# Norm chain with fewer and reordered steps, and a shared area padded to a 128-byte base

## The chip, the cores and the metric

The kernel runs on one core of a Trainium2 chip. The metric is the device time of one execution in microseconds; the times given are medians of runs. The core has a matmul engine (TensorE, PE), a vector engine (DVE), a scalar engine (ACT), a GpSimd engine (POOL) and a sync engine (SP) whose queue issues most transfers. Each works through its own list of instructions in order and waits for the others by semaphores.

## The reference

Everything is float32, T = 512 tokens, width D = 1024. The first block has two layers; each layer has a feed-forward, a mixer and a feed-forward, each behind a norm, and a final norm follows. The second block has a hybrid of attention and a gated linear recurrence, and an MLP, each behind a norm.

```
rms_norm(x, g)       = x * rsqrt(mean(x * x, -1) + 1e-6) * g
modulate(h, sh, sc)  = h * (1 + sc) + sh            # sh, sc, gate from silu(c) @ ada_w + ada_b
swiglu(h)            = (silu(a) * b) @ w_out,  [a | b] = h @ w_in        # inner width 2816
layer 0: ffn, pool_mixer (trailing means over 2, 4, 8, 16 tokens, then a 256x256 map per group), ffn
layer 1: ffn, conv_mixer (h @ w_in, causal 3-tap convolution, @ w_out), ffn
x = x + 0.5 * gate * swiglu(modulate(rms_norm(x, g), sh, sc))            # the mixers: without 0.5
```

## The kernel before

Activations lie transposed: the residual `X` is eight tiles of 128 channels by 512 tokens, all in on-chip memory. Every product with a weight is exact float32 from three passes: weight and activation are each split into a rounded high half and the rest, and `products` issues high x high, high x low and low x high (L1382 to L1384). A *unit* of weights is up to 1024 rows by 256 columns. SP loads unit u into `W_RAW[u % 2]` once unit u-2 has been split (L393, L397); ACT rounds it into `W_HI` (`split_hi`, L529) once the products of unit u-2 are over; DVE subtracts (`split_lo`, L773) and so frees the raw buffer; PE multiplies. In a feed-forward a half is 11 input units and 8 output units (`IN_UNITS`, `OUT_UNITS`); each input unit has 48 products of 512 columns (8 tiles of `H_HI`, `H_LO` by 2 column blocks by 3 passes).

There are nine norms, r = 0 to 8: 0 ahead of the first feed-forward, 1 ahead of the pool mixer, 2, 3 ahead of feed-forwards, 4 ahead of the convolution, 5 ahead of the last feed-forward, 6 the final norm of the first block, 7 and 8 in the second block. A norm goes through four engines:

- ACT squares the eight tiles of `X` into two buffers (`squares`, L536); DVE copies the first into `SSQ` (L833) and adds the others (L836), each addition behind the one before. In front of norms 1, 3, 4 and 6 tiles 0 to 6 are squared and summed during the last two output units (`EARLY`); only tile 7 is left. In front of norms 5 and 8 two tiles are left, in norms 2 and 7 nearly all.
- PE reduces `SSQ` over channels: four column products of one column each (`norm`, L1394). They are plain float32 and appear as 8 instructions.
- ACT takes the root (`root`, L540). The table of the root and that of Silu are different ones; a table load of its own (ACT_TABLE_LOAD) precedes a function whose table isn't there.
- DVE takes the reciprocal (L841) and makes four diagonal tiles (L846); PE multiplies ones with them (L1397, two instructions), which spreads the 512 factors over all partitions.
- For each tile k DVE forms x * gain * factor into `GT[k % 2]` (`normed`, L852), ACT adds the shift into `SA[k % 2]` (L548) and rounds it into `H_HI` (L551), DVE subtracts into `H_LO` (`lo`, L859), and the first unit's products of tile k may start. DVE's order is normed 0, normed 1, lo 0, normed 2, lo 1, and so on.

The order around it is written by hand. The unit that the first products need is split already. The unit after it (`ahead`) is rounded by ACT between the last square and the root, and subtracted by DVE between the last sum and the reciprocal, in norms 2 to 5 and likewise in norm 1. In norm 1 DVE then shifts the tiles in place (L935), forms the trailing means (L944 to L956), splits them (L960), and adds the mixer's result to `X` (L876); PE starts the third of four groups (L1437) when the first group's addition is done. Ahead of norm 1's root ACT also takes Silu of the two other condition vectors (L592).

Many buffers of different stages share one area, `FLEX`, by offsets: `G_HI`, `G_LO`, `ADA`, `SA`, `GT`, `PH` and those of the second block.

## Time and profile before

| | us |
|---|---|
| median of three timed runs | 3264.14 |
| lowest and highest of them | 3259.08, 3264.15 |
| the profiled execution | 3260.7 |
| its span, first to last instruction | 3258.7 |
| busy in it: PE, DVE, ACT | 2849.9, 1579.4, 870.9 |

The mean granted clock of PE was 0.921 of full speed. Rows of the timeline give start, duration, engine, line and operation, and in brackets how long the engine had been idle before and who released it. PE's products overlap: one of 512 columns lasts longer than the distance to the next.

### The profile page before, as it was taken

How to read it: one execution, taken by the hardware profiler on the slowest of the kernel's cores; microseconds unless marked ns; L12 is line 12 of the kernel's file. 1: busy time of each engine (PE TensorE's matmuls, PEld its weight loads, DVE VectorE, ACT ScalarE, POOL GpSimd, SP SyncE). 2: the span in 40 equal slices, each digit the busy share in tenths (PEclk: the TensorE clock that was granted, in tenths of full speed). 3: DMA queues.
4: the chain of work that ended last, by engine and by line, in shares of the span. 5: the costliest groups of instructions: out<-in, count | busy, mean ns of one | idle time of the engine just before them, and what ended most of it. 6: DMA issues, size and time to landing. Idle time of an engine off the chain costs nothing.

```text
span 3258.7 us, 33240 instructions
## 1 busy us (share of the span) xinstructions
PE 2849.9 (87%) x12574; PEld 2321.7 (71%) x12574; DVE 1579.4 (48%) x2135; ACT 870.9 (27%) x937; POOL 65.6 (2%) x132
## 2 busy tenths in 40 slices
PE   4999939999899998989999478877666669989999
PEld 3888828888788887878887366766544448778887
DVE  5636476455563844556343555355323243354444
ACT  3212223221322223231222333333122243332221
POOL 0100000000000000000000000000000000000000
PEclk9999969999999999999999678877877789999999
DMA  6746415455373643236342201001100003323232
GB/s 235 233 121 207 123 51 167 150 162 189 92 238 107 214 128 85 96 97 213 109 131 75 63 27 39 27 27 42 31 13 13 13 26 90 90 78 100 93 103 78
DMA packets 418458, 340.17 MB, mean 104 GB/s; under 512 B 11328, under 2 KB 399936, under 8 KB 410048
## 3 DMA queue, kind: packets, MB, share of 16 engines
q1 hardware_dynamic: 400368, 244.84, 25.6%
q0 software_dynamic: 17568, 93.33, 7.7%
q8 instruction: 63, 1.03, 0.1%
q10 hardware_dynamic: 432, 0.75, 0.1%
q14 instruction: 27, 0.22, 0.0%
HBM read 336.78 MB, written 2.10 MB: 104 GB/s over the span
## 4 chain that ended last, share of the span: by engine, by line
PE 84%; DVE 9%; ACT 3%; issue 2%; SPq 1%; DMA 0%; DVEq 0%; ACTq 0%
PE ps L1382 23%; PE ps L1383 23%; PE ps L1384 23%; PE ps L1476 3%; PE ps L1478 3%; PE ps L1477 3%; PE ps L1650 2%; PE ps L1640 1%; DVE gla_kql L1154 1%; SPq L393 1%; DVE stat L1275 1%; ACT w_hi L529 1%; PE ps L1397 1%; DVE gla_el L1139 1%; DVE attn_p L1285 0%
## 5 line engine op out<-in xcount | busy, mean ns | idle before, releaser
L1382 PE MATMUL ps<-h_hi,w_hi 128*128 128x512 f32 x2256 | 894.2, 396 | 39.5 <-DVE h_lo L859 18.8
L1383 PE MATMUL ps<-h_lo,w_hi 128*128 128x512 f32 x2256 | 888.7, 394 | 0.0
L1384 PE MATMUL ps<-h_hi,w_lo 128*128 128x512 f32 x2256 | 887.8, 394 | 0.0
L773 DVE TENSOR_TENSOR w_lo<-w_raw,w_hi 128x2048 fp32r<-128x2048 f32 (+1 forms) x240 | 504.7, 2103 | 201.2 <-ACT w_hi L529 200.8
L529 ACT CAST w_hi<-w_raw 128x2048 fp32r<-128x2048 f32 (+1 forms) x240 | 421.9, 1758 | 617.0 <-PE ps L1384 554.4
L1382 PEld LDWEIGHTS ps<-h_hi,w_hi 128*128 128x128 f32 x2256 | 430.9, 191 | 147.8 <-issue 58.1
L1383 PEld LDWEIGHTS ps<-h_lo,w_hi 128*128 128x128 f32 x2256 | 430.7, 191 | 91.0 <-issue 1.5
L1384 PEld LDWEIGHTS ps<-h_hi,w_lo 128*128 128x128 f32 x2256 | 430.1, 191 | 91.2
L1382 PE MATMUL ps<-g_hi,w_hi 128*128 128x512 f32 x960 | 373.4, 389 | 0.0
L1383 PE MATMUL ps<-g_lo,w_hi 128*128 128x512 f32 x960 | 373.4, 389 | 0.0
L1384 PE MATMUL ps<-g_hi,w_lo 128*128 128x512 f32 x960 | 373.4, 389 | 0.0
L876 DVE SCALAR_TENSOR_TENSOR x_res<-ps,gate,x_res 128x512 f32<-128x512 f32 (+1 forms) x120 | 87.4, 749 | 401.3 <-PE ps L1384 395.2
L566 ACT ACTIVATE silu_a<-ps 128x512 f32<-128x512 f32 x88 | 52.7, 599 | 730.9 <-PE ps L1384 730.9
L891 DVE TENSOR_TENSOR g_t<-silu_a,ps 128x512 f32<-128x512 f32 x88 | 60.6, 688 | 360.8 <-ACT silu_a L566 360.8
L778 DVE SCALAR_TENSOR_TENSOR ada<-ada,cond 128x1024 f32<-128x1024 f32 x176 | 207.7, 1220 | 0.3 <-DMA ada<-in_ada_t 0.2
L1383 PEld LDWEIGHTS ps<-g_lo,w_hi 128*128 128x128 f32 x960 | 180.2, 188 | 37.5
L1384 PEld LDWEIGHTS ps<-g_hi,w_lo 128*128 128x128 f32 x960 | 180.2, 188 | 37.4
L1382 PEld LDWEIGHTS ps<-g_hi,w_hi 128*128 128x128 f32 x960 | 180.2, 188 | 37.3
L1558 PE MATMUL ps<-gla_kql 128*128 128x128 f32 x224 | 56.8, 439 | 38.5 <-DVE gla_kql L1154 38.5
L1558 PEld LDWEIGHTS ps<-gla_kql 128*128 128x128 f32 x224 | 49.7, 327 | 46.0 <-DVE gla_kql L1154 46.0
L1640 PE MATMUL ps<-ident,attn_p 128*128 128x128 f32 x192 | 37.5, 354 | 49.6 <-DVE attn_p L1285 49.6
L1394 PE MATMUL ps<-ones_d,ssq 128*128 128x1 f32 x72 | 14.3, 320 | 75.8 <-DVE ssq L836 75.8
(264 smaller groups left out, 2624.5 us busy)
## 6 DMA issues: line engine op xcount, KB each, us to landing
w_raw<-in_ffn_w_in SPq DMA_DIRECT2D x176, 512.0 KB, 5.0
ada<-in_ada_t POOLq DMA_DIRECT2D x56, 1024.0 KB, 6.5
ada<-in_ada_t POOLq DMA_DIRECT2D x64, 512.0 KB, 5.3
w_raw<-in_w_mlp SPq DMA_DIRECT2D x64, 512.0 KB, 4.3
w_raw<-in_w_in SPq DMA_DIRECT2D x52, 512.0 KB, 4.6
w_raw<-in_ffn_w_out SPq DMA_DIRECT2D x64, 384.0 KB, 4.1
w_raw<-in_ffn_w_out SPq DMA_DIRECT2D x64, 320.0 KB, 3.4
w_raw<-in_conv_w_in SPq DMA_DIRECT2D x24, 512.0 KB, 4.4
```

Source lines behind the costliest of these rows:

```text
L529: nc.scalar.copy(W_HI[u.slot][:, 0:n], W_RAW[u.slot][:, 0:n]).then_inc(hi_done, 1)
L773: nc.vector.tensor_tensor(W_LO[u.slot][:, 0:n], W_RAW[u.slot][:, 0:n], W_HI[u.slot][:, 0:n].bitcast(F32), ALU.subtract).then_inc(lo_done, 1)
L778: return nc.vector.scalar_tensor_tensor(tile, tile, 1.0, COND[cond][:], ALU.mult, ALU.mult, accum_out=MOD_SUMS[:, bass.ds(n.v, 1)])
L876: return nc.vector.scalar_tensor_tensor(x, bank[:], GATE[:, bass.ds((m + 8 * gate).v, 1)], x, ALU.mult, ALU.add)
L1382: pe.matmul(dst, hi[:, k, c], rhs_hi(k), start=(k == 0), stop=False)
L1383: pe.matmul(dst, hi[:, k, c], rhs_lo(k), start=False, stop=False)
L1384: last = pe.matmul(dst, lo[:, k, c], rhs_hi(k), start=False, stop=(k == kt - 1))
L1476: pe.matmul(dst, a_hi, b_hi, start=first, stop=False)
L1477: pe.matmul(dst, a_hi, b_lo, start=False, stop=False)
L1478: return pe.matmul(dst, a_lo, b_hi, start=False, stop=last)
L1558: last = pe.matmul(BANK[6 + n % 2][:, cc], KQL[n % 2][:, 0, cc], KQL[n % 2][:, 1, cc], start=True, stop=True)
L1640: last = pe.transpose(WIDE[2 * (c % 2)][:, t * P:(t + 1) * P], PP[c % 2][:, t * P:(t + 1) * P], IDENT[:])
```

## The change

1. The weight unit `ahead` is rounded by ACT behind tile 3 of the norm's loop, and subtracted by DVE behind normed 5 and lo 4. In norm 1 ACT takes the root first and then rounds; DVE subtracts behind the pool's last low half and ahead of the residual additions.
2. The first two squares are added in one operation (no copy), and tile 7 is left out of `SSQ`. PE multiplies `SSQ` (tiles 0 to 6) when it is ready, and then the square of tile 7 from its own buffer into the same columns: 8 column products instead of 4.
3. Behind the last square ACT takes a root of one column into a spare column of `RSTD4`, whose table load so comes there.
4. The four diagonal tiles are one operation over 128x512 with broadcast operands.
5. ACT adds the shift while it rounds into `H_HI`; DVE's `lo` adds it again in a two-step operation (SCALAR_TENSOR_TENSOR). `SA` is no longer between them; `NT = GT + SA` gives four buffers for the normed tiles.
6. `RSTD4` is four columns wider, and ahead of `FLEX` a pad brings its base to a multiple of 128 bytes.

```
@@ -199,10 +199,13 @@
         MODS = sb("mods", [P, N_MODS + 16])
         GAIN = sb("gain", [P, 9 * KD])
         GATE = sb("gate", [P, 8 * KD])
-        RSTD4 = sb("rstd4", [P, 8])
+        RSTD4 = sb("rstd4", [P, 12])
         DIAG = sb("diag", [P, 4, P])
         SSQ = sb("ssq", [P, T])
         FLEX_KB = 86
+        PAD = -nc.sbuf_base % 128
+        if PAD:
+            sb("pad", [P, PAD // 4])
         FLEX = sb("flex", [P, FLEX_KB * 256])
         FLEX0 = nc.sbuf_base - FLEX_KB * 1024
 
@@ -220,6 +223,7 @@
         COND = [view(f"cond{n}", 56 + 4 * n, [P, D]) for n in range(3)]
         SA = [view(f"silu_a{s}", 68 + 2 * s, [P, T]) for s in range(2)]
         GT = [view(f"g_t{s}", 72 + 2 * s, [P, T]) for s in range(2)]
+        NT = GT + SA
 
         PH = view("pool_h", 0, [P, KD, T])
         PS_A = view("pool_a", 16, [P, 2, T])
@@ -368,6 +372,7 @@
         def vecs(name, a, b):
             return VECS[:, VEC_COLS[name][0] + a:VEC_COLS[name][0] + b]
 
+        SUMS = KD - 2
         FFN_GROUPS = [(1, 2), (3, 4), (5, 6), (7, 8)]
         FFN_NORM = [0, 2, 3, 5]
         FFN_NEXT = [1, 3, 4, 6]
@@ -532,23 +537,24 @@
 
                 for k in tiles:
                     ready(k)
-                    wait(act, sq_summed, at(KD * r + k - 1))
+                    if k >= 2:
+                        act.wait_ge(sq_summed, SUMS * r + max(k - 2, 1))
                     nc.scalar.activation((SA if r == 7 else GT)[k % 2][:], X[:, k, :], ACT.Square).then_inc(sq_made, 1)
+                if KD - 1 in tiles:
+                    nc.scalar.activation(RSTD4[:, 8:9], EPS_C[:], ACT.Sqrt)
 
             def root(r):
                 act.wait_ge(ms_made, r + 1)
                 nc.scalar.activation(RSTD4[:, 4:8], BANK[6][:, 0:4], ACT.Sqrt, bias=EPS_C[:]).then_inc(rt_made, 1)
 
-            def h_hi(r, g):
+            def h_hi(r, g, ahead=None):
 
                 for k in range(KD):
                     act.wait_ge(xr_made, KD * r + k + 1)
-                    if k >= 2:
-                        act.wait_ge(h_ready, H_BASE[r] + k - 1)
-                    nc.scalar.activation(SA[k % 2][:], GT[k % 2][:], ACT.Identity,
-                                         bias=MODS[:, 24 * g + k:24 * g + k + 1]).then_inc(h_made, 1)
-                    act.wait_ge(h_made, KD * (r - (r > 6)) + k + 1)
-                    nc.scalar.copy(H_HI[:, k, 0:T], SA[k % 2][:]).then_inc(h_hi_made, 1)
+                    nc.scalar.activation(H_HI[:, k, 0:T], NT[k % 4][:], ACT.Identity,
+                                         bias=MODS[:, 24 * g + k:24 * g + k + 1]).then_inc(h_hi_made, 1)
+                    if ahead is not None and k == 3:
+                        split_hi(at(ahead))
 
             def after_ffn(f):
                 return lambda k: act.wait_ge(evac_done, U_FFN[f] + FFN_UNITS - OUT_UNITS + k + 1)
@@ -590,24 +596,21 @@
             act.wait_ge(cond_2_landed, 32)
             for n in range(2):
                 nc.scalar.activation(COND[n + 1][:], COND[n + 1][:], ACT.Silu).then_inc(cond_ready, 1)
+            root(1)
             split_hi(at(U_POOL + 1))
-            root(1)
             for k in range(KD):
                 act.wait_ge(pool_mixed, k + 1)
                 nc.scalar.copy(H_HI[:, k, 0:T], PH[:, k, :]).then_inc(p_hi_made, 1)
             squares(2, lambda k: act.wait_ge(pool_added, k // 2 + 1) if k < 6 else
                     act.wait_ge(evac_done, U_POOL + 1))
-            split_hi(at(U_FFN[1] + 1))
             root(2)
-            h_hi(2, 2)
+            h_hi(2, 2, U_FFN[1] + 1)
             ffn(1)
-            split_hi(at(U_FFN[2] + 1))
             root(3)
-            h_hi(3, 3)
+            h_hi(3, 3, U_FFN[2] + 1)
             ffn(2)
-            split_hi(at(U_CONV + 1))
             root(4)
-            h_hi(4, 4)
+            h_hi(4, 4, U_CONV + 1)
 
             def cv_unit(j):
                 u = j + U_CONV
@@ -621,9 +624,8 @@
             each(act, 4, 0, 0, lambda j: split_hi(j + (U_CONV + 9)))
             each(act, 4, 0, 2, lambda j: split_hi(j + (U_CONV + 13)))
             squares(5, lambda k: act.wait_ge(evac_done, U_CONV + 12 + k // 2 + 1))
-            split_hi(at(U_FFN[3] + 1))
             root(5)
-            h_hi(5, 5)
+            h_hi(5, 5, U_FFN[3] + 1)
             ffn(3)
 
             root(6)
@@ -826,13 +828,15 @@
                 last.then_inc(mod_done, 1)
 
             def square_sums(r, tiles=range(KD)):
+
                 sq = SA if r == 7 else GT
                 for k in tiles:
-                    dve.wait_ge(sq_made, KD * r + k + 1)
-                    if k == 0:
-                        nc.vector.tensor_copy(SSQ[:], sq[0][:]).then_inc(sq_summed, 1)
-                    else:
-                        dve.wait_ge(sq_summed, KD * r + k)
+                    if k == 1:
+                        dve.wait_ge(sq_made, KD * r + 2)
+                        nc.vector.tensor_tensor(SSQ[:], sq[0][:], sq[1][:], ALU.add).then_inc(sq_summed, 1)
+                    elif 2 <= k < KD - 1:
+                        dve.wait_ge(sq_made, KD * r + k + 1)
+                        dve.wait_ge(sq_summed, SUMS * r + k - 1)
                         nc.vector.tensor_tensor(SSQ[:], SSQ[:], sq[k % 2][:], ALU.add).then_inc(sq_summed, 1)
 
             def rstd_diag(r):
@@ -842,8 +846,8 @@
                 dve.wait_ge(rs_made, r + 1)
                 if r == 0:
                     dve.wait_ge(tab_landed, 16)
-                for c in range(4):
-                    nc.vector.tensor_scalar(DIAG[:, c, :], IDENT[:], RSTD4[:, c:c + 1], None, ALU.mult).then_inc(diag_made, 1)
+                nc.vector.tensor_tensor(DIAG[:], IDENT[:].rearrange("p (c t) -> p c t", c=1).broadcast_to([P, 4, P]),
+                                        RSTD4[:, 0:4].rearrange("p (c t) -> p c t", t=1).broadcast_to([P, 4, P]), ALU.mult).then_inc(diag_made, 1)
 
             def normed(r, k, dst, gain):
 
@@ -856,17 +860,19 @@
 
                 def lo(k):
                     dve.wait_ge(h_hi_made, H_BASE[r] + k + 1)
-                    nc.vector.tensor_tensor(H_LO[:, k, 0:T], SA[k % 2][:], H_HI[:, k, 0:T].bitcast(F32),
-                                            ALU.subtract).then_inc(h_ready, 1)
+                    nc.vector.scalar_tensor_tensor(H_LO[:, k, 0:T], NT[k % 4][:], MODS[:, 24 * g + k:24 * g + k + 1],
+                                                   H_HI[:, k, 0:T].bitcast(F32), ALU.add, ALU.subtract).then_inc(h_ready, 1)
                 square_sums(r, tiles)
-                if ahead is not None:
-                    split_lo(at(ahead))
                 rstd_diag(r)
                 dve.wait_ge(mod_done, g + 1)
                 for k in range(KD):
-                    normed(r, k, GT[k % 2][:], GAIN[:, 8 * g + k:8 * g + k + 1])
+                    if k >= 4:
+                        dve.wait_ge(h_ready, H_BASE[r] + k - 3)
+                    normed(r, k, NT[k % 4][:], GAIN[:, 8 * g + k:8 * g + k + 1])
                     if k >= 1:
                         lo(k - 1)
+                    if ahead is not None and k == 5:
+                        split_lo(at(ahead))
                 lo(KD - 1)
 
             def add_branch(m, bank, gate):
@@ -925,8 +931,6 @@
             norm_split(0, 0, None, ())
             ffn(0)
 
-            square_sums(1, (KD - 1,))
-            split_lo(at(U_POOL + 1))
             rstd_diag(1)
             dve.wait_ge(mod_done, 2)
             for k in range(KD):
@@ -937,7 +941,7 @@
             steps = 0
             for gi, w in enumerate(POOL_WINDOWS):
                 h = PH[:, 2 * gi:2 * gi + 2, :]
-                dve.wait_ge(h_made, KD + 2 * gi + 2)
+                dve.wait_ge(h_made, 2 * gi + 2)
                 src, dst, s = h, PS_A, 1
                 while s < w:
 
@@ -959,6 +963,7 @@
                     dve.wait_ge(p_hi_made, k + 1)
                     nc.vector.tensor_tensor(H_LO[:, k, 0:T], PH[:, k, :], H_HI[:, k, 0:T].bitcast(F32),
                                             ALU.subtract).then_inc(p_ready, 1)
+            split_lo(at(U_POOL + 1))
             for gi in range(4):
                 if gi < 3:
                     dve.wait_ge(pool_mm, gi + 1)
@@ -1029,7 +1034,6 @@
             norm_split(5, 5, U_FFN[3] + 1, (6, 7))
             ffn(3)
 
-            square_sums(6, (KD - 1,))
             rstd_diag(6)
             for k in range(KD):
                 normed(6, k, X[:, k, :], vec("final_g", k))
@@ -1389,11 +1393,15 @@
 
             def norm(r):
 
-                pe.wait_ge(sq_summed, KD * (r + 1))
+                pe.wait_ge(sq_summed, SUMS * (r + 1))
                 for c in range(4):
-                    last = pe.matmul(BANK[6][:, c:c + 1], SSQ[:, c * P:(c + 1) * P], ONES_D[:, 0:1], start=True, stop=True)
+                    pe.matmul(BANK[6][:, c:c + 1], SSQ[:, c * P:(c + 1) * P], ONES_D[:, 0:1], start=(c == 0), stop=False)
+                pe.wait_ge(sq_made, KD * (r + 1))
+                sq = (SA if r == 7 else GT)[(KD - 1) % 2]
+                for c in range(4):
+                    last = pe.matmul(BANK[6][:, c:c + 1], sq[:, c * P:(c + 1) * P], ONES_D[:, 0:1], start=False, stop=(c == 3))
                 last.then_inc(ms_made, 1)
-                pe.wait_ge(diag_made, 4 * (r + 1))
+                pe.wait_ge(diag_made, r + 1)
                 pe.matmul(BANK[5][:], ONES[:], DIAG[:].rearrange("p c t -> p (c t)"), start=True, stop=True).then_inc(rb_made, 1)
 
             def ffn(f):
```

## Rows read from the trace of the kernel before

**Rows 1.** The page, part 1: busy time, share of the span, instructions of each engine.

```profile
PE 2849.9 (87%) x12574; PEld 2321.7 (71%) x12574; DVE 1579.4 (48%) x2135; ACT 870.9 (27%) x937; POOL 65.6 (2%) x132
```

**Rows 2.** Chain of waits, TensorE: total us, times, longest.

```profile
PE ps L1394 <- DVE ssq L836: 75.8, 9, 40.8
```

**Rows 3.** Timeline, norm 3: start us, us, engine line operation [idle before, releaser].

```profile
853.24 1.88 ACT L529 CAST w_hi<-w_raw 128x2048 fp32r<-128x2048 f32 x1
...
854.12 1.05 PE L1394 MATMUL ps<-ones_d,ssq 128*128 128x1 f32 x8 [2.23 <-DVE ssq L836]
855.14 1.28 ACT L540 ACT_TABLE_LOAD   x1
855.16 2.29 DVE L773 TENSOR_TENSOR w_lo<-w_raw,w_hi 128x2048 fp32r<-128x2048 f32 x1 [1.10 <-ACT w_hi L529]
856.44 0.26 ACT L540 ACTIVATE rstd<-ps,eps_c 128x4 f32<-128x4 f32 x1
...
857.57 0.88 DVE L846 TENSOR_SCALAR diag<-ident,rstd 128x128 f32<-128x128 f32 x4
...
858.50 2.07 PE L1397 MATMUL ps<-diag,ones 128*128 128x512 f32 x2 [3.33 <-DVE diag L846]
860.68 1.41 DVE L852 SCALAR_TENSOR_TENSOR g_t<-x_res,gain,ps 128x512 f32<-128x512 f32 x2 [2.24 <-PE ps L1397]
861.47 0.72 ACT L548 ACTIVATE silu_a<-g_t,mods 128x512 f32<-128x512 f32 x1 [4.76 <-DVE g_t L852]
862.22 0.62 ACT L551 CAST h_hi<-silu_a 128x512 fp32r<-128x512 f32 x1
...
862.87 0.69 DVE L859 TENSOR_TENSOR h_lo<-silu_a,h_hi 128x512 fp32r<-128x512 f32 x1 [0.78 <-ACT h_hi L551]
...
863.71 0.76 PE L1382 MATMUL ps<-h_hi,w_hi 128*128 128x512 f32 x1 [3.13 <-DVE h_lo L859]
```

**Rows 4.** Stretches: length, busy of PE, PEld, DVE, ACT, POOL; PEclk, DMA share, GB/s.

```profile
851.80:856.70 4.90, 1.14 (x9) 0.97 (x8) 2.99 (x3) 3.96 (x4) 0.00 (x0) 1.00 0.46 126
863.70:867.00 3.30, 3.29 (x8) 2.62 (x9) 3.14 (x6) 3.00 (x5) 0.00 (x0) 0.50 0.02 5
876.00:886.00 10.00, 10.00 (x45) 8.29 (x45) 4.02 (x4) 2.40 (x2) 0.00 (x0) 1.00 0.35 100
1236.40:1242.40 6.00, 5.97 (x14) 4.80 (x15) 5.67 (x9) 5.59 (x9) 0.00 (x0) 0.50 0.00 1
```

**Rows 5.** Timeline, norm 2.

```profile
475.45 5.47 DVE L836 TENSOR_TENSOR ssq<-ssq,g_t 128x512 f32<-128x512 f32 x7
...
480.98 1.87 PE L1394 MATMUL ps<-ones_d,ssq 128*128 128x1 f32 x8 [7.41 <-DVE ssq L836]
481.88 2.29 DVE L773 TENSOR_TENSOR w_lo<-w_raw,w_hi 128x2048 fp32r<-128x2048 f32 x1 [0.95 <-ACT w_hi L529]
```

**Rows 6.** Timeline, norm 1 and the end of the pool stage.

```profile
415.91 1.99 ACT L592 ACTIVATE cond<-cond 128x1024 f32<-128x1024 f32 x2
...
425.00 0.26 ACT L540 ACTIVATE rstd<-ps,eps_c 128x4 f32<-128x4 f32 x1
...
427.07 2.08 PE L1397 MATMUL ps<-diag,ones 128*128 128x512 f32 x2 [8.42 <-DVE diag L846]
...
463.47 2.72 DVE L876 SCALAR_TENSOR_TENSOR x_res<-ps,gate,x_res 128x512 f32<-128x512 f32 x4
```

**Rows 7.** Timeline, norm 5.

```profile
1415.79 1.49 DVE L836 TENSOR_TENSOR ssq<-ssq,g_t 128x512 f32<-128x512 f32 x2 [0.70 <-ACT g_t L536]
...
1418.10 2.29 DVE L773 TENSOR_TENSOR w_lo<-w_raw,w_hi 128x2048 fp32r<-128x2048 f32 x1 [0.82 <-ACT w_hi L529]
```

**Rows 8.** Timeline, norm 7: the first normed and the last low half.

```profile
1811.36 1.41 DVE L852 SCALAR_TENSOR_TENSOR g_t<-x_res,gain,ps 128x512 f32<-128x512 f32 x2 [2.23 <-PE ps L1397]
...
1823.19 0.69 DVE L859 TENSOR_TENSOR h_lo<-silu_a,h_hi 128x512 fp32r<-128x512 f32 x1 [0.58 <-ACT h_hi L551]
```

**Rows 9.** The page, part 6: transfers issued, KB each, us to landing.

```profile
w_raw<-in_ffn_w_in SPq DMA_DIRECT2D x176, 512.0 KB, 5.0
```

More of the change, by code:

```diff
@@ L866, in norm_split @@
                 for k in range(KD):
-                    normed(r, k, GT[k % 2][:], GAIN[:, 8 * g + k:8 * g + k + 1])
+                    if k >= 4:
+                        dve.wait_ge(h_ready, H_BASE[r] + k - 3)
+                    normed(r, k, NT[k % 4][:], GAIN[:, 8 * g + k:8 * g + k + 1])
                     if k >= 1:
                         lo(k - 1)
+                    if ahead is not None and k == 5:
+                        split_lo(at(ahead))
                 lo(KD - 1)
@@ L1030, in _ @@
             ffn(3)
-            square_sums(6, (KD - 1,))
             rstd_diag(6)
```

74 lines of the change are left out of this document (39 added, 35 removed).

## The prediction

> **What bounds the kernel now.** I read the page first: the matmul engine is busy for 87% of the span [rows 1], so time is won only where it stands still or runs at the low clock. The chain of waits of that engine says where it stands still around the change [rows 2]: the longest is for the vector engine's running sum, 75.8 us over nine norms, of which 40.8 are the start of the program. Inside the feed-forward blocks, behind their first unit, the same view has no wait of this engine for the others, so what a norm in front of a block gains or loses goes straight to the end. Then I followed one norm after the other in the timeline. Norms are numbered as in the code, 0 to 8.
>
> Norm 3 is the pattern [rows 3]. The last product before it ends at 854.12 - 2.23 = 851.9 us. The column products that reduce the squares (8 instructions) run at 854.12. Meanwhile the scalar engine rounds the next weight unit (853.24, 1.88 us), and only behind that loads the root table (855.14) and takes the root. The vector engine subtracts that unit (855.16, 2.29 us) and only behind that makes the diagonal tiles (857.57). So the two weight splits, not the column products, set the start of the broadcast product at 858.50. The first normed tile starts at t0 = 860.68, the first product of the next unit at 863.71, 3.03 us behind t0.
>
> The clock matters too [rows 4]: the granted clock is at full speed (2.4 GHz) in the 4.9 us behind the last product, up to 856.7, is half (1.2 GHz) when the products start again, and is full again after about 3.2 us of products in norm 3 and about 6.0 us in norm 4. A 512-column product starts every 0.43 us at the low clock (14 in 6.0 us) and every 0.22 to 0.23 us at the high one (45 in 10.0 us); I use 0.227. A low stretch of c us costs 0.47 c.
>
> **Norms 3 and 4** (norm 4 has the same timeline). New order: the first four column products take the sum of tiles 0 to 6 and start when the engine stops, 851.9 to 852.95. The square of tile 7 is done at 853.3; the second four take it directly, 853.4 to 854.45 (8 instructions again 1.05 us, clock still high). The table load moves up to 853.24 and ends at 854.5, the small extra root costs between nothing and the 0.26 of the real one, I take 0.2, so the root runs 854.7 to 855.0. Reciprocal, 0.2 with its gap. The diagonal becomes one two-input operation over 512 columns: not in the trace in this form, but a subtraction over 512 columns takes 0.69 [rows 3], the four small ones 0.88; between 0.69 and 0.88 I take 0.69. Broadcast product at 855.9 instead of 858.5: **2.6 us earlier**.
>
> Behind t0: before, the first tile needed normed 0.74, shift 0.72, rounding 0.62, subtraction 0.69 and hand-overs, 3.03 together. The shift now happens in the rounding and again in the subtraction, which becomes a two-step operation (0.74 like L852). 0.74 + 0.05 + 0.72 + 0.03 + 0.74 + 0.15 = 2.43: the products start 0.6 us sooner. But the splits are now inside this loop. The vector engine starts an operation every 0.67 us; tile 3 leaves the scalar engine at t0+5.1; the weight rounding holds it to t0+7.0; tile 4 leaves it at 7.6, its low half is done at 8.4; the weight subtraction runs 8.3 to 10.5; normed tile 6; and the low half of tile 5 is done at t0+11.9. The matmul engine needs it after 30 products, at 2.43 + 6.8 + 0.47 c = t0+10.7 to 12.0 for c of 3.2 to 6.0. It waits up to 1.3 us, and the unit's 48 products end at t0+12.0+18x0.227 = 16.1 whatever the clock did. Before they ended at 3.03 + 10.9 + 0.47 c = t0+15.4 to 16.8, mean 16.1. **So the 0.6 us are given back: 0 in this part**, and norms 3 and 4 gain 2.6 us each, 5.2 together.
>
> **Norms 2 and 5.** Here the sum itself is late and the first four column products can't hide. Norm 2 [rows 5]: seven dependent additions at 0.80 us from 475.45, end 480.9; 8 column instructions 1.87 (low clock); the split ended 484.17 and set the reciprocal. New: no copy, the first addition starts at 474.9 and six of them end at about 480.3; now 16 instructions at the low clock, 3.7 us, end 484.0. The broadcast product starts at 485.3 instead of 485.2: nothing gained. Norm 5 [rows 7]: the sum without tile 7 is ready at 1416.5, 16 instructions end between 1418.6 (clock high) and 1420.2 (low), a root and 0.3 us later comes the reciprocal; now it comes at 1420.3, when the subtraction started at 1418.10 lets go: between 1.3 gained and 0.2 lost, I take 0.4 gained. Loop part as above, 0.
>
> **Norm 1 (pool)** [rows 6]. The chain now is: a weight transfer, its rounding, table load, root at 425.00, weight subtraction, diagonals, broadcast product 427.07. New: the root no longer sits behind the transfer. But the early table load comes ahead of the two Silu operations on the conditions (415.91, 1.99 us), which then need their own table back, and the root a third load: 416.0 + 1.3 + 0.2 + 1.3 + 2.0 + 1.3 = 422.1, root to 422.4, product at 423.2: 3.9 us earlier. The moved weight subtraction (2.2 us) is now queued on the vector engine ahead of the pool's residual additions (463.47), and those release the matmul engine's third group: 2.2 lost. Net 1.7. The Trainium skill, page "ScalarE: Activation LUTs", section "What ACT_TABLE_LOAD costs", says that a switch of table is a load and a drain behind it, about 2.66 us together, and advises to group functions by set. The trace shows the load at 1.28 and the root 0.02 behind it (855.14 and 856.44 in norm 3 by the timeline), no drain; by the page's price the three loads would take 4.1 us more in norm 1, and the gain there would be gone.
>
> **The others.** Norm 0: the chain through the first weight transfers, splits and modulation is untouched up to the diagonals; these save 0.2, the first tile 0.6, and no split is in the loop: 0.8. Norm 6 has no split; the table load and the small root now end later than the column products, so it saves about 0.4 of its sum's last addition and 0.2 on the diagonals: 0.6. Norm 7 [rows 8] is like norm 2 without a split: 8 more column instructions cost 1.8, an addition and the copy less save 1.3, the diagonals 0.2, and its loop, where all eight tiles must be ready, shrinks from 1823.88 - 1811.36 = 12.5 us to about 11.2 (16 operations at 0.67 and two short waits), 1.3: together 1.0, of which I keep 0.8 for the hand-overs. Norm 8 starts its column products one addition sooner (0.8) but issues 8 more, 1.05 to 1.86 us by the clock; diagonals 0.2 and first tile 0.6 stand against it: 0.1.
>
> **The padding.** By the declared sizes the shared area starts at a multiple of 128 bytes now; the four added columns would move it off, the pad puts it back to such a multiple. Tiles inside it keep their place relative to each other, so I cost it at nothing.
>
> **Sum.** 0.8 (norm 0) + 1.7 (1) + 0 (2) + 5.2 (3, 4) + 0.4 (5) + 0.6 (6) + 0.8 (7) + 0.1 (8) = 9.6 us. The profiled execution took 3260.7 us: 3251.1. The median of the three timed runs is 3264.1, their lowest 3259.1: taken from the median 3254.5. The median is what the change will be held against, less a little for the profiled run below it: **3254 us**.
>
> **Rivals.** (a) *The split in the loop starves the matmul engine more than I count.* If tiles 5 to 7 come another 1.4 us late (hand-overs, or a two-step subtraction dearer than 0.74: its bounds are the 0.69 of one step and the 1.48 of two L852, and at 1.1 the six of them up to tile 5 would be 2 us later), four norms lose 5.6: 3260, no measurable change. For: the margin in the loop is nil by my own count. Against: all rows of the operations are steady to 0.01 us. (b) *The clock stays high through the shorter gap of norms 3 and 4*, or is back sooner: each saves 0.47 x 3.2 to 6.0 and up to 1 us of the broadcast product, about 3.5 each: 3247. Against: it was high for 4.9 us after the last product and low at 863.7 [rows 4], and the new gap is still about 8.5 us with only small work in it. (c) *Slower:* the moved weight subtraction frees its raw buffer some 10 us later, and the transfer queue, which is in order, starts the unit after next later. It starts at t0+10.6, takes about 5 us [rows 9], and the rounding wants it at about t0+27. The slack is 10 us; only if such a load took over 15 us in each of the norms 2 to 5, and over 19 us (4 us of idling each) would the gain of 9.6 be undone; 20 us and more makes it over 0.2% slower, 3272. The engines of the transfers are quiet there (share 0.02 [rows 4]), so this is unlikely. (d) *The padding moves time:* nearly every product of the feed-forward's second half reads this area; 1% on them would be some 11 us either way. Nothing in the rows speaks for it.
>
> **How the numbers follow.** Forecast 0.62, (a) 0.20, (b) 0.12, (c) 0.04, (d) 0.02. A measurement of this kernel tells about 0.2% (6.5 us) from no change: its own three runs differ by 5 us. The forecast's edge towards "no change" is 3 us away, so I leave it 0.09 there. Faster 0.53 + 0.12 + 0.01 = 0.66, same 0.09 + 0.20 = 0.29, slower 0.05. Range: the bounds of the unknown costs are small beside the spread of executions; from (b) at 3247 to just over (a), 3261.
>
> **What the new profile would show.** Column products of norm 3 in two groups, the first right at the stop, the broadcast product some 4 us behind the stop instead of 6.6; the first product of the unit 2.4 us behind t0; a wait of about 1 us of the matmul engine for the low half of tile 5 in norms 2 to 5; three table loads between 416 and 422; the pool's additions behind a weight subtraction. The prediction is wrong if the wait for tile 5 is well over 1 us, if the clock falls or rises elsewhere, or if the gap in norm 3 is set by something else than the root.

## The result and the profile after

The changed kernel takes 3279.74 us (median of 14 runs, 3266.46 to 3292.77), the kernel before 3261.99 us in 14 runs beside it (3258.47 to 3268.77). The ratio is 1.0049, with a 95% interval of 1.0035 to 1.0062. The change makes the kernel slower by 0.5%. I had forecast 3254 us and gave "slower" a chance of 0.05. The profiled execution of the changed kernel took 3269.57 us (span 3267.8) at a mean granted clock of 0.924.

**The norms do what the prediction said.** This is norm 3 in the timeline of the changed kernel. The columns are those of [rows 3].

```profile
854.23 0.95 PE L1398 MATMUL ps<-ones_d,ssq 128*128 128x1 f32 x8
854.43 0.75 DVE L882 SCALAR_TENSOR_TENSOR x_res<-ps,gate,x_res 128x512 f32<-128x512 f32 x1 [2.01 <-PE ps L1388]
855.21 0.63 ACT L542 ACTIVATE g_t<-x_res 128x512 f32<-128x512 f32 x1 [5.47 <-DVE x_res L882]
855.86 1.28 ACT L544 ACT_TABLE_LOAD   x1
...
855.89 1.05 PE L1402 MATMUL ps<-ones_d,g_t 128*128 128x1 f32 x8 [0.72 <-ACT g_t L542]
857.15 0.20 ACT L544 ACTIVATE rstd<-eps_c 128x1 f32<-128x1 f32 x1
857.26 0.25 ACT L548 ACTIVATE rstd<-ps,eps_c 128x4 f32<-128x4 f32 x1
857.54 0.18 DVE L845 RECIPROCAL rstd<-rstd 128x4 f32<-128x4 f32 x1 [2.36 <-ACT rstd L548]
857.75 0.69 DVE L849 TENSOR_TENSOR diag<-ident,rstd 128x512 f32<-128x512 f32 x1
...
858.50 2.07 PE L1405 MATMUL ps<-diag,ones 128*128 128x512 f32 x2 [1.55 <-DVE diag L849]
860.68 1.41 DVE L856 SCALAR_TENSOR_TENSOR g_t<-x_res,gain,ps 128x512 f32<-128x512 f32 x2 [2.23 <-PE ps L1405]
...
863.12 0.76 PE L1386 MATMUL ps<-h_hi,w_hi 128*128 128x512 f32 x1 [2.54 <-DVE h_lo L863]
...
868.82 2.29 DVE L775 TENSOR_TENSOR w_lo<-w_raw,w_hi 128x2048 fp32r<-128x2048 f32 x1
```

The last product ahead of the norm ends at 854.39 in the record, and the first half of the column products has started at 854.23, with no wait. The second half waits for the last square (855.84). The table load runs beside it. The broadcast product starts at 858.50, 4.11 us behind the end of that last product; before it was 858.50 - 851.89 = 6.61 behind [rows 3]. The first product comes 863.12 - 860.68 = 2.44 us behind the first normed tile, before 3.03. The weight subtraction sits inside the loop, 8.1 us behind the first normed tile. The starts of the broadcast product happen to carry the same number, 858.50, in both traces. By then the new chain had saved 2.5 us in this norm and, as the first experiment will show, 3.4 us ahead of it, and something else had cost as much.

**The products became slower.** These groups of instructions by line and shape (busy us, mean ns of one) are the kernel before:

```profile
L1382 PE MATMUL ps<-h_hi,w_hi 128*128 128x512 f32 x2256 | 894.2, 396 | 39.5 <-DVE h_lo L859 18.8 <-DVE attn_vs L1246 11.7 <-DVE h_lo L1317 3.7
L1382 PE MATMUL ps<-g_hi,w_hi 128*128 128x512 f32 x960 | 373.4, 389 | 0.0
L1382 PE MATMUL ps<-z_hi,w_hi 128*128 128x512 f32 x64 | 24.9, 389 | 0.0
```

and the same groups of the changed kernel:

```profile
L1386 PE MATMUL ps<-h_hi,w_hi 128*128 128x512 f32 x2256 | 895.8, 397 | 35.4 <-DVE h_lo L863 16.5 <-DVE attn_vs L1250 11.7 <-DVE h_lo L1321 3.7
L1386 PE MATMUL ps<-g_hi,w_hi 128*128 128x512 f32 x960 | 379.2, 395 | 0.0
L1386 PE MATMUL ps<-z_hi,w_hi 128*128 128x512 f32 x64 | 25.3, 395 | 0.0
```

The moving tile of the first group is `H_HI`, outside the shared area, and it costs the same. `G_HI` and `z_hi` lie in the shared area, and each of their products lasts 6 ns longer. The lines L1387 and L1388 of these tiles show the same 395. There are 3 x 960 products of `g` in the feed-forwards, 3 x 64 of `z` in the convolution, and in the second block 3 x 64 of `l` and as many of `a`, 3456 in all. So a loss of 6 ns is spread over every feed-forward and shows up in no wait at all. In the page the matmul engine is busy 31.8 us more than in [rows 1]. Some 21 us of that are these four groups, and some 11 are the column products, which were 14.3 us and are 25.6:

```profile
PE 2881.7 (88%) x12646; PEld 2331.3 (71%) x12646; DVE 1569.8 (48%) x2090; ACT 840.0 (26%) x892; POOL 65.6 (2%) x132
```

In the chain of waits the line that answers to [rows 2] is shorter by 15 us, which is more than the kernel can have gained: the column products that take `SSQ` now begin earlier.

```profile
PE ps L1398 <- DVE ssq L840: 60.6, 5, 37.3
```

**Where the area lies.** The declared sizes give the addresses. The weight and H buffers outside the shared area (`W_HI`, `W_LO`, `H_HI`, `H_LO`, and every slice of 128 columns or more that a product takes of them) start 128 bytes past a multiple of 256. `FLEX` started at 139,904, also 128 past a multiple of 256. It now starts at 140,032, which is a multiple of 256. In the kernel before the `g`, `z`, `l` and `a` tiles and the weights had the same place within 256 bytes; in the changed kernel they have not.

### The profile page after: what moved, and what is told of

Its sections match the earlier page's. It is cut to its first block, busy times and chain, and to the rows that moved or that the text cites. A ratio compares the mean times of both kernels' runs of the same rounds, so it can differ in the third digit from the quotient of the medians.

```text
span 3267.8 us, 33218 instructions
## 1 busy us (share of the span) xinstructions
PE 2881.7 (88%) x12646; PEld 2331.3 (71%) x12646; DVE 1569.8 (48%) x2090; ACT 840.0 (26%) x892; POOL 65.6 (2%) x132
## 3 DMA queue, kind: packets, MB, share of 16 engines
q1 hardware_dynamic: 400368, 244.84, 25.6%
## 4 chain that ended last, share of the span: by engine, by line
PE 84%; DVE 9%; ACT 3%; issue 2%; SPq 1%; DMA 0%; DVEq 0%; ACTq 0%
PE ps L1386 23%; PE ps L1387 23%; PE ps L1388 23%; PE ps L1484 3%; PE ps L1486 3%; PE ps L1485 3%; PE ps L1658 2%; PE ps L1648 1%; DVE gla_kql L1158 1%; DVE stat L1279 1%; SPq L398 1%; DVE gla_el L1143 1%; PE ps L1405 1%; ACT w_hi L534 1%; DVE h_lo L863 0%
## 5 line engine op out<-in xcount | busy, mean ns | idle before, releaser
L1387 PE MATMUL ps<-h_lo,w_hi 128*128 128x512 f32 x2256 | 889.0, 394 | 0.0
L1388 PE MATMUL ps<-h_hi,w_lo 128*128 128x512 f32 x2256 | 887.9, 394 | 0.0
L1387 PEld LDWEIGHTS ps<-h_lo,w_hi 128*128 128x128 f32 x2256 | 431.0, 191 | 91.5 <-issue 2.1
L1388 PEld LDWEIGHTS ps<-h_hi,w_lo 128*128 128x128 f32 x2256 | 430.3, 191 | 90.8
L1388 PE MATMUL ps<-g_hi,w_lo 128*128 128x512 f32 x960 | 379.2, 395 | 0.0
L1387 PE MATMUL ps<-g_lo,w_hi 128*128 128x512 f32 x960 | 379.1, 395 | 0.0
L1387 PEld LDWEIGHTS ps<-g_lo,w_hi 128*128 128x128 f32 x960 | 180.2, 188 | 43.8
L1388 PEld LDWEIGHTS ps<-g_hi,w_lo 128*128 128x128 f32 x960 | 180.2, 188 | 43.8
L1484 PE MATMUL ps<-w_hi,h_hi 128*128 128x256 f32 x240 | 70.5, 294 | 0.0
```

Of the source, the lines that this page charges most:

```text
L1387: pe.matmul(dst, hi[:, k, c], rhs_lo(k), start=False, stop=False)
L1388: last = pe.matmul(dst, lo[:, k, c], rhs_hi(k), start=False, stop=(k == kt - 1))
L1484: pe.matmul(dst, a_hi, b_hi, start=first, stop=False)
```

## The experiments

Two numbers are given for most runs. The median is held against the kernel before on the same chip. The other is the span of the profiled execution less one stretch of it, from the end of the second block's first unit to the stop ahead of norm 8, which holds the recurrence and the attention. That stretch takes 1041.0 us in the trace before and between 1038 and 1059 in the others, with hardly any change of its own in the edits; the last section comes back to it. The rest of the span is steadier: 2217.7 us before, 2226.7 after, +9.0. It comes from one execution of each kernel. Part of what it varies by is the start of the program: in nine traces with the new norm chain the first weight product starts between 50.36 and 51.94 us, in three with the old chain between 52.07 and 52.75. So a difference of 1 us or so between two kernels says little.

**The norm edits alone, at the old addresses.** `RSTD4` keeps its eight columns, no pad, and the extra root writes elsewhere.

```
-        RSTD4 = sb("rstd4", [P, 12])
+        RSTD4 = sb("rstd4", [P, 8])
-        PAD = -nc.sbuf_base % 128
-        if PAD:
-            sb("pad", [P, PAD // 4])
-        STAT = sb("stat", [P, 64])
+        STAT = sb("stat", [P, 72])
-                    nc.scalar.activation(RSTD4[:, 8:9], EPS_C[:], ACT.Sqrt)
+                    nc.scalar.activation(STAT[:, 64:65], EPS_C[:], ACT.Sqrt)
```

> All edits of the norm chain, but the extra root goes to a spare column behind the shared area, so RSTD4 stays 8 columns wide, no pad is needed, and every tile keeps the address that it had before (shared area at byte 139,904). Theory A (the new base of the shared area, 140,032, costs each 512-column product that streams a tile of it 0.233 instead of 0.227 us, 3456 such products, 23 us; the norm chain itself gains): these products are back at 0.227 and the time is 3262 - 10 = 3252 us, ratio to before 0.997. Theory B (the norm chain, or its other order, is what makes it slower): 3270 us or more, ratio 1.003 or more, and products as slow as in the changed kernel.

Measured: 3249.9 us (3244.78 to 3266.81, 8 runs) against 3263.72 before; ratio 0.996, interval 0.9947 to 0.9973. Theory A had said 3252. Outside the stretch the span is 2208.2 us, 9.5 below before. The products of `g` are back at 389 ns:

```profile
L1383 PE MATMUL ps<-g_hi,w_hi 128*128 128x512 f32 x960 | 373.6, 389 | 0.0
```

**The addresses alone, in the kernel before.** This is the other half of the change: `RSTD4` twelve wide and the pad, the norms untouched.

```
-        RSTD4 = sb("rstd4", [P, 8])
+        RSTD4 = sb("rstd4", [P, 12])
+        PAD = -nc.sbuf_base % 128
+        if PAD:
+            sb("pad", [P, PAD // 4])
```

> The kernel before with only the wider RSTD4 and the pad, so that every tile has the address of the changed kernel; the norm chain is the old one. Theory A: 3456 products at 0.233 us, 3262 + 23 = 3285 us, ratio 1.007. Theory B: 3262 us, no change.

Measured: 3289.95 us (3287.44 to 3290.7, 5 runs); ratio 1.0078, interval 1.0065 to 1.0091. Theory A had said 3285. Outside the stretch 2237.0 us, +19.3.

```profile
L1386 PE MATMUL ps<-g_lo,w_hi 128*128 128x512 f32 x960 | 379.3, 395 | 0.0
```

The two halves add up within the uncertainty of the start: -9.5 and +19.3 make +9.8, and the changed kernel shows +9.0. That leaves no room for another cost outside the stretch.

**The changed kernel with the area 128 bytes further on.** The base becomes 140,160, which is at the weights' place within 256 bytes again. Everything else of the change stays.

```
-        PAD = -nc.sbuf_base % 128
+        PAD = -nc.sbuf_base % 128 + 128
```

> The changed kernel with 128 bytes more of pad: the shared area starts at 140,160, an odd multiple of 128 as before, instead of an even one. Theory A in the form that the address within 256 bytes decides: 0.227 us per product, about 3252 us. Rival within A (what was moved ahead of the shared area, the diagonal tiles and the sum by 32 bytes, or any other base than the old one): 0.233 us and about 3280 us. Theory B: about 3280 us too.

Measured: 3249.3 us (3241.73 to 3262.03, 12 runs); ratio 0.9964, interval 0.995 to 0.9977. Outside the stretch 2208.2 us, the same as with the norm edits alone.

```profile
L1386 PE MATMUL ps<-g_hi,w_hi 128*128 128x512 f32 x960 | 373.6, 389 | 0.0
```

One number in one line turns a change that loses 17.8 us in the median into one that gains 14.4, each against the kernel before on its own chip.

**The price by itself.** This kernel leaves all of the reference's work out (its output is its input). It issues groups of 30 products of 512 columns, each with one place of the moving tile and one of the stationary tile.

```
+        OFFS = [o for n in range(16) for o in (32 * n, 32 * n + 512)]
+        GROUPS = [(mov(o), stat(96)) for o in OFFS]
+        for m in (0, 128, 256):
+            for s in (0, 32, 64, 128, 160, 256, 384):
+                GROUPS.append((mov(m), stat(s)))
+            for n, (m, s) in enumerate(GROUPS):
+                for i in range(30):
+                    last = pe.matmul(BANKS[n % 7][:], s, m, start=True, stop=True)
```

> A kernel that leaves out all the work: the output is the input. It streams one 512-column tile 30 times for each of 32 start addresses (0 to 992 in steps of 32 bytes behind a multiple of 4096) against one fixed stationary tile (96 behind such a multiple), then moving starts 0, 128, 256 against stationary starts 0, 32, 64, 128, 160, 256, 384. Theory A, moving start within 256 bytes: 0.233 us at 0, 256, 512, 768 and 0.227 at 128, 384, 640, 896 and at 224. Rival: the distance between the moving and the stationary tile decides, then the second part changes with the stationary start. Theory B: all the same.

Measured, in the timeline of that kernel. The stationary tile lies at 96 bytes; from the top, the moving tile lies at 64, 576, 96, 608, 128, 640, 160, 672 and 192 (all behind a multiple of 4096). The start of a row less that of the row before it is the time of 30 products.

```profile
52.11 7.16 PE L227 MATMUL bank_e<-area 128*128 128x512 f32 x30
59.11 7.16 PE L227 MATMUL bank_f<-area 128*128 128x512 f32 x30
66.11 6.99 PE L227 MATMUL bank_g<-area 128*128 128x512 f32 x30
72.93 6.96 PE L227 MATMUL bank_a<-area 128*128 128x512 f32 x30
79.73 7.16 PE L227 MATMUL bank_b<-area 128*128 128x512 f32 x30
86.73 7.16 PE L227 MATMUL bank_c<-area 128*128 128x512 f32 x30
93.73 7.04 PE L227 MATMUL bank_d<-area 128*128 128x512 f32 x30
100.61 7.03 PE L227 MATMUL bank_e<-area 128*128 128x512 f32 x30
107.48 7.17 PE L227 MATMUL bank_f<-area 128*128 128x512 f32 x30
```

At 64 and 576 it is 7.00 us, at 96 and 608 it is 6.82 and 6.80 (608 is 96 plus twice 256), at 128 and 640 again 7.00, at 160 and 672 it is 6.88 and 6.87. The other 23 places up to 992 repeat this every 256 bytes: 6.82 and 6.80 at 352 and 864, 6.88 and 6.87 at 416 and 928, and 7.00 to 7.03 at the rest. The second part moves both tiles. These are the us of 30 products:

| moving tile at | stationary at 0 | 32 | 64 | 128 | 160 | 256 | 384 |
|---|---|---|---|---|---|---|---|
| 0 | 6.85 | 6.99 | 7.00 | 6.97 | 7.00 | 6.84 | 6.99 |
| 128 | 6.97 | 7.00 | 6.88 | 6.83 | 6.99 | 6.97 | 6.81 |
| 256 | 6.81 | 6.99 | 7.00 | 6.97 | 7.00 | 6.85 | |

The fast cells are those where both tiles start at the same place within 256 bytes: 0.227 to 0.228 us for one product. All others take 0.232 to 0.234, except where the moving tile is 64 bytes further on, which takes 0.229. So theory A as put for this run, a slow place of the moving tile by itself, is wrong, and its rival, the distance between the two tiles, is right. In the kernels' own traces the products of `g` start every 0.2267 us at the old address and every 0.2333 at the new one. The difference is 6.7 ns, or 2.9%. By it the 2880 products of `g` and the 192 of `z`, all outside the stretch, cost 3072 x 0.00667 = 20.5 us. The run with the addresses alone showed 19.3, in a trace whose first product came 0.7 us early. The 384 of `l` and `a` would add 2.6 us inside the stretch.

**Both moved.** To tell the relative place from the absolute one in the kernel itself: 128 bytes ahead of all tiles, and the area at 140,288. Weights and area are now both at multiples of 256, where the changed kernel's slow area was.

```
+        sb("front", [P, 32])
         W_RAW = [sb(f"w_raw{s}", [P, FULL]) for s in range(2)]
-        PAD = -nc.sbuf_base % 128
+        PAD = -nc.sbuf_base % 128 + 128
```

> The changed kernel with 128 bytes ahead of all tiles, so that weights and H tiles start at even multiples of 128 (W_RAW at 16,640), and 128 more ahead of the shared area, now at 140,288, an even multiple too. Theory A1 (a product is fast when moving and stationary tile start at the same place within 256 bytes): both are at 0 of 256, all products 0.227 us, 3250 us. Theory A2 (a moving tile at a multiple of 256 bytes is slow as such): the products with H tiles become slow as well, 0.233 for nearly all, 3280 + 45 = 3325 us.

Measured: 3247.8 us (3239.45 to 3267.59, 10 runs) against 3263.86; ratio 0.9955, interval 0.9939 to 0.997; outside the stretch 2206.6, -11.1. It is the relative place that counts.

```profile
L1388 PE MATMUL ps<-g_hi,w_hi 128*128 128x512 f32 x960 | 373.6, 389 | 0.0
```

**Without the pad.** The wider `RSTD4` stays, so the base falls to 139,936, 32 bytes past the old one.

```
-        PAD = -nc.sbuf_base % 128
-        if PAD:
-            sb("pad", [P, PAD // 4])
```

> The changed kernel without the pad: the shared area starts at 139,936, 32 bytes past the place within 256 where the weights start. By the sweep (moving 128 against stationary 96) its products take 0.233 us, as with the pad, and the time is that of the changed kernel, about 3280 us. Rival: only a base that is an even multiple of 128 is slow, then 0.227 and 3250.

Measured: 3275.42 us in the one run taken, outside the stretch 2227.5, +9.8. The pad is neither the cure nor the culprit: the four columns alone put the area 32 bytes off the weights' place, and the pad moved it to another place that is no better. Of the bases tried only those that agree with the weights are fast.

```profile
L1384 PE MATMUL ps<-g_hi,w_hi 128*128 128x512 f32 x960 | 379.4, 395 | 0.0
```

**What the moved splits are worth.** The norm edits alone, with the weight splits back ahead of root and reciprocal.

```
-                    if ahead is not None and k == 3:
-                        split_hi(at(ahead))
+            split_hi(at(U_FFN[2] + 1))
             root(3)
```

(and likewise in norms 1, 2, 4, 5, and for `split_lo`)

> The kernel of the first experiment (old base) with the weight splits back ahead of root and reciprocal, all other edits of the norm chain kept. If the splits were what set the start of the broadcast product in norms 3 and 4, it is back at 6.6 us or later behind the last product (the extra root now stands ahead of the split: up to 7), and 3250 + 6 = 3256 us. Rival: fewer steps alone give the gain, then it stays at 4.3 us and 3250.

Measured: 3270.19 us (3254.86 to 3279.36, 10 runs); ratio 1.0013, interval 0.9994 to 1.0032. The expectation was 3256. Outside the stretch 2216.8 us, 0.9 below before and 8.6 above the norm edits alone. In norm 3 the broadcast product starts 7.95 us behind the end of the last product, later than the 6.61 before the change: the small root and its table load then sit ahead of the weight rounding and delay it.

```profile
856.91 2.07 PE L1404 MATMUL ps<-diag,ones 128*128 128x512 f32 x2 [5.39 <-DVE diag L848]
```

So without the moved splits the shorter steps bring 0.9 us, and with them 9.5. That does not make 8.6 us the worth of the order alone: 1.3 us in norm 3 and again in norm 4 come of the small root ahead of the rounding, which the kernel before does not have.

**Splits later still.** The prediction's loop count said that a split behind tile 3 takes back what the shift gives. Here the ahead split goes behind tile 7, the pool's weight subtraction between the second and third group's additions, and norm 1 has no extra root.

```
-                    if ahead is not None and k == 3:
+                    if ahead is not None and k == KD - 1:
-            split_lo(at(U_POOL + 1))
             for gi in range(4):
+                if gi == 2:
+                    split_lo(at(U_POOL + 1))
```

> The kernel of the first experiment (old base) with three things moved: the next weight unit is split behind tile 7 of the loop instead of inside it, the pool stage's weight subtraction stands between the second and the third group's additions instead of ahead of the first, and norm 1 has no extra root. If the loop's accounting holds, the wait for tile 5 goes (about 0.6 us in each of four norms), the pool additions come 2.2 us sooner, and norm 1's root 2.8 sooner: 3250 - 7.4 = 3242 us, ratio 0.9935. Rival: the unit's end is set by the clock, not by tile 5, and the pool stage by its own chain: 3248 or more.

Measured: 3254.85 us (3238.52 to 3264.52, 12 runs); ratio 0.9974, interval 0.9963 to 0.9985. The expectation was 3242, and the median missed it by 13 us. Outside the stretch 2198.3 us, 19.4 below before and 9.9 below the norm edits alone; the expectation had said 7.4 below. From the end of the last product ahead of it to the end of the next 48 products norm 1 takes 52.35 us instead of 56.59 with the norm edits alone, norm 3 20.95 instead of 22.51, norm 4 20.87 instead of 22.65 and norm 5 24.02 instead of 25.47. In norm 3 the broadcast product also ran at the high clock (its window has a granted clock of 1.00, in the changed kernel 0.50):

```profile
848.08 1.12 PE L1403 MATMUL ps<-diag,ones 128*128 128x512 f32 x2 [1.55 <-DVE diag L846]
```

The 9.9 us are not in the median, which is 5 us above that of the norm edits alone. Its profiled execution was its fastest (3238.52), and had the stretch at 1038.5. The others probably lost their time in the stretch: the next two kernels differ from this one by a few additions that, as will be seen, hold nothing up. Their profiled executions took 3257.87 and 3247.00 us, and have 2197.2 and 2198.5 us outside the stretch and 1059.0 and 1046.7 in it.

**A delay that didn't arrive.** The aim was to see whether the stretch's time hangs on when its work starts. At its start, behind the second block's first unit, the vector engine is given additions that depend on each other and whose result nothing reads.

```
             dve.wait_ge(pe_done, U_LR + 1)
+            for n in range(3):
+                nc.vector.tensor_tensor(SSQ[:], X[:, 0, :], X[:, 1, :], ALU.add).then_inc(late, 1)
+                dve.wait_ge(late, n + 1)
```

First the kernel before with three, meant as 2.4 us (they took 2.2):

> The kernel before, with three additions of 512 columns (0.8 us each, result unused) that hold up the second block once, behind its first weight unit: 2.4 us. The question is the spread of 25 us and more that the new norm chain shows where the old one shows 12. Theory P: the stretch of recurrence and attention takes 1037 to 1065 us by how the granted clock's changes fall against its short gaps, and what goes before shifts that; then this delay moves the time of the stretch by more than itself, or widens it. Rival: the stretch takes what it takes, the spread comes with the new chain's code; then the time is 3264 + 2.4 = 3266 us with the old spread.

Measured: 3267.23 us (3261.91 to 3268.93, 10 runs) against 3265.88; ratio 1.0004, interval 0.9995 to 1.0014. Then the kernel with later splits, with three and with six (meant as 4.8 us; they took 4.4):

> The kernel with the later splits (3255 us in the median, although 9.9 us faster than the first experiment's kernel outside that stretch) with the same delay of 2.4 us. Theory P: the stretch, 1055 us in its median, moves by several us against the 2.4 of the delay, possibly down: 3245 to 3262. Rival: 3257 us.

> The same with a delay of 4.8 us. Theory P: yet another median of the stretch, not 2.4 us more than with the delay of 2.4. Rival: 3260 us.

Measured: 3257.07 us (3248.91 to 3264.79, 10 runs), ratio 0.9978, interval 0.9964 to 0.9991; and 3253.16 us (3242.36 to 3263.75, 6 runs), ratio 0.9963, interval 0.9943 to 0.9982. The traces show why these runs can't answer the question. First the kernel with later splits without additions, then with six:

```profile
1844.82 0.69 DVE L1168 COPY gla_kq<-ps 128x512 f32<-128x512 f32 x1 [9.54 <-PE ps L1484]
...
1846.58 1.55 PE L1526 MATMUL ps<-low_rank,w_gk 32*128 32x512 f32 x4 [1.80 <-DVE gla_kq L1170]
```

```profile
1831.55 4.33 DVE L1072 TENSOR_TENSOR ssq<-x_res 128x512 f32<-128x512 f32 x6 [7.43 <-PE ps L1488]
...
1845.30 0.69 DVE L1172 COPY gla_kq<-ps 128x512 f32<-128x512 f32 x1 [6.19 <-PE ps L1488]
...
1847.07 1.55 PE L1530 MATMUL ps<-low_rank,w_gk 32*128 32x512 f32 x4 [1.80 <-DVE gla_kq L1174]
```

The vector engine had 9.5 us of idle time there, waiting for the next unit's products, and the additions only filled part of it. The matmul engine's first wait for the vector engine ends 15.6 us behind the first unit (which ends at 1831.01 and 1831.51) in both, and just so in the other two kernels with additions. No product behind it was held up, so these are in effect two more samples of the kernel with later splits, with medians 2.2 above and 1.7 below its own, and one of the kernel before. Theory P was not tested.

## Why the prediction was wrong

**The step that failed** is the section on the padding: "Tiles inside it keep their place relative to each other, so I cost it at nothing". True, and not what counts: a product reads a tile inside the area and a weight outside it, and their places relative to each other did change. It costs 20.5 us outside the stretch by the price of one product (measured +19.3 with the addresses alone; in the changed kernel +9.0 where the norm edits alone have -9.5) and some 2.6 inside. Rival (d) named where it would show, "1% on them would be some 11 us either way", but gave no mechanism, and I gave it 0.02. Its price was mis-worked too: 11 us are 1% of the busy times of the `g` products (3 x 373.4 us), which overlap; from start to start 1% of them is 2880 x 0.227 x 0.01 = 6.5 us. The true size was 2.9%. "Nothing in the rows speaks for it" was an argument only as far as rows could speak. In the trace before all these products had their two tiles at the same place within 256 bytes, so it could not show what another place costs. An unmeasured cost on nearly 3000 instructions of the engine that sets the end deserved more than one time in fifty.

The Trainium skill, page "SBUF — State Buffer", section "Operand start alignment", asks of an operand only that it start at a multiple of its element size, and says that this is about legality, not speed. The runs show a speed beside it: every place tried here is allowed, and most distances between the two tiles cost some 2.9%.

**The norms, term by term.** The kernel with the norm edits alone tells them without the addresses. How far the end of the matmul engine's last product ahead of a norm, or its first product behind it, has moved against the trace before gives each term:

| norm | forecast us | measured us | read from |
|---|---|---|---|
| 0 | 0.8 | 0.8 | first product 52.75 to 51.94 |
| 1 and 2 | 1.7 + 0 | 2.6 | shift at norm 3's stop, 3.4 |
| 3 | 2.6 | 2.1 | shift at norm 4's stop, 5.5 |
| 4 | 2.6 | 3.2 | shift at norm 5's stop, 8.7 |
| 5 | 0.4 | 0.4 | shift at norm 6's stop, 9.1 |
| 6 and 7 | 0.6 + 0.8 | 0.0 | shift at the end of the next unit, 9.1 |
| 8 | 0.1 | 0.4 | rest of the span, 367.4 to 367.0 |

The sum is 9.5, forecast were 9.6. That it is so near is in part luck: some terms were mis-sized and cancel, and the first carries the start's variation. Norms 6 and 7 had gained 1.1 us when the next unit's products began (1840.47 to 1830.32), and that unit gave it back: it took 10.9 us instead of 9.8. In norm 1 the time from the last product to the broadcast product shrank by 3.7 us, near the 3.9 worked out, but the pool gave back only about 1.2 instead of 2.2; norm 2 gained 0.1. The three table loads forecast for norm 1 are there in the changed kernel:

```profile
417.77 1.28 ACT L544 ACT_TABLE_LOAD   x1
...
419.07 0.20 ACT L544 ACTIVATE rstd<-eps_c 128x1 f32<-128x1 f32 x1
419.27 1.28 ACT L598 ACT_TABLE_LOAD   x1
420.57 2.00 ACT L598 ACTIVATE cond<-cond 128x1024 f32<-128x1024 f32 x2
422.59 1.28 ACT L548 ACT_TABLE_LOAD   x1
423.88 0.27 ACT L548 ACTIVATE rstd<-ps,eps_c 128x4 f32<-128x4 f32 x1
...
425.14 2.07 PE L1405 MATMUL ps<-diag,ones 128*128 128x512 f32 x2 [6.28 <-DVE diag L849]
```

Each load takes 1.28 us, and the function behind it starts 0.01 to 0.02 us later. The gain in norm 1 was not lost. The 2.66 us of the page "ScalarE: Activation LUTs" of the Trainium skill, section "What ACT_TABLE_LOAD costs", don't hold here.

**The loop.** The forecast let the split in the loop take back what the earlier first product gives, with a wait for tile 5 of up to 1.3 us. In norm 3 of the changed kernel tile 5's low half was written from 871.68 to 872.43, and the first product of that tile starts at 872.48. It and the next come some 0.2 us late in all, so the forecast's wait of about 1 us did not show. The matmul engine was itself late, because the clock was low for 4.8 us there:

```profile
863.10:867.90 4.80, 4.79 (x11) 3.78 (x12) 4.49 (x7) 3.64 (x4) 0.00 (x0) 0.50 0.00 0
```

The balance was right all the same. The unit's 48 products end at 876.91, 16.2 us behind the first normed tile, and the forecast was 16.1. With the split out of the loop they take 0.6 us less in norm 3 and 1.0 us less in norm 4, from the first product to the end of the last. The rest of the 1.6 and 1.8 us that these norms gain there lies ahead of the first product, mostly in a broadcast product at the high clock. Rival (a), starvation, is out. Rival (b), the clock staying high, happens now and then: the broadcast product took 2.07 us in norm 3 of the changed kernel and 1.12 in that of the kernel with later splits. Rival (c), transfers made late, did not show.

**How the total comes about.** Outside the stretch -9.5 + 19.3 = +9.8, measured +9.0. The median is 17.8 us above before. Of the other 8.8, some 2.6 are the slower products inside the stretch. The rest, about 6, is a longer stretch in the median execution, and its cause stays open. By the timed runs the kernel with the addresses alone has a longer stretch too, by 7 us in its median and 2.6 by its products, so the addresses may have a part in it; the kernels with later splits have it long at the old addresses. The forecast's range did not allow for it; the three runs of the kernel before, from which it took its spread, lay 5 us apart.

## What to carry to other kernels

Two tiles that the matmul engine reads together are to be compared by their addresses, not only by their sizes: when an edit widens any buffer ahead of them, work out both starts modulo 256 bytes again. A rounding to 128 bytes isn't enough. If a group of instructions that the edit doesn't touch shows another mean in the table by line and shape, compare that before any wait; no wait shows it. And where a cost that no row could show falls on thousands of instructions of the engine that sets the end, it belongs in the range with its full product.

## What the runs showed of the hardware that was not expected

**The 256-byte relation.** A product of 512 fp32r columns at the high clock takes 0.227 us from start to start when moving and stationary tile start at the same place within 256 bytes, 0.229 when the moving tile is 64 bytes further on, and 0.232 to 0.234 at the other distances tried. Why is not known; only starts at multiples of 32 bytes and one shape were tried.

**A stretch whose time varies with the granted clock.** Between the first unit of the second block and norm 8 the matmul engine works in short pieces, and the granted clock there is well below one. The columns are those of [rows 4]. First the kernel before, then the changed one, the norm edits alone, and the kernel with later splits:

```profile
1850.10:2891.10 1041.00, 815.32 (x3742) 653.08 (x3740) 418.49 (x632) 316.33 (x381) 0.00 (x0) 0.83 0.14 40
```

```profile
1854.10:2895.30 1041.20, 817.28 (x3742) 652.92 (x3740) 418.14 (x631) 316.19 (x381) 0.00 (x0) 0.83 0.14 40
```

```profile
1841.00:2898.00 1057.00, 832.34 (x3742) 665.23 (x3740) 417.89 (x631) 316.08 (x381) 0.00 (x0) 0.82 0.14 40
```

```profile
1830.80:2869.30 1038.50, 813.66 (x3742) 651.12 (x3740) 418.15 (x631) 316.22 (x381) 0.00 (x0) 0.84 0.14 40
```

The same 3742 matmul instructions are busy for 814 to 832 us, while the vector and scalar engines' busy times agree within 0.6 us. A lower clock goes with a longer stretch. If the time outside it is taken as steady, the timed runs put it at 1037 to 1049 us in the kernel before (median 1044), 1038 to 1064 in the changed one (1051), 1035 to 1057 with the norm edits alone (1040) and 1038 to 1065 with later splits (1055). With the addresses alone it is 1048 to 1052 (1051), in the two other kernels with the new chain and agreeing places 1032 to 1052 (1039) and 1031 to 1059 (1040), and with the splits back 1036 to 1061 (1052). So every kernel with the new norm chain that ran more than once spreads over 16 us or more there, and those with the old chain over 3 to 12. Why the new norm chain, whose work lies mostly outside this stretch, should widen the spread there stays open. It matters for what can be claimed: the version with later splits is the best outside the stretch, by 9.9 us against the norm edits alone, and yet not in its median. The lowest medians, 3247.8 to 3249.9 us, are those of the norm edits alone and of the two kernels that moved the area back to the weights' place; all three lie below both the kernel before and the changed one.
